# A two-layer fp32 transformer with a sparse third layer: turning between stages by token tile, and inverse roots of the attention heads on VectorE

## The reference, cut to what matters

```
def rms_norm(x, g):
    return x * rsqrt(mean(x * x, -1) + EPS) * g

for i in range(2):
    a = mixer(rms_norm(h, norm_g[i, 0]))              # mla_mixer, then diff_mixer
    h = h + rms_norm(a, norm_g[i, 1])
    f = conv_ffn(rms_norm(h, norm_g[i, 2]))
    h = h + rms_norm(f, norm_g[i, 3])
h = hybrid_layer(h)                                   # begins with rms_norm(h, g_mix)

# in diff_mixer, for each of 8 heads, o is [256, 128]:
    p = softmax(q0 @ k0.T - bias) - lam * softmax(q1 @ k1.T - bias)
    o = rms_norm(p @ v, subln_g) * (1 - lam_init)
```

## Time and profile before

| | us |
|---|---|
| median of 3 runs | 1344.09 |
| lowest, highest | 1343.32, 1346.96 |
| the profiled execution, its time | 1345.34 |
| the profiled execution, its span | 1343.5 |
| TensorE busy in it | 1282.8 |
| GpSimd, ScalarE, VectorE busy | 573.2, 548.0, 509.6 |
| mean granted TensorE clock | 0.994 |

### The profile page before, as it was taken

How to read it: one execution, slowest core, us unless ns; L and a number is a source line. 1 busy time by engine, 2 the same in 40 slices (tenths; PEclk the granted TensorE clock), 3 DMA queues, 4 the chain that set the end, 5 groups by cost and what they waited for, 6 DMA issues and landing times.

```text
span 1343.5 us, 20032 instructions
## 1 busy us (share of the span) xinstructions
PE 1282.8 (95%) x7959; PEld 954.6 (71%) x7959; DVE 509.6 (38%) x1303; ACT 548.0 (41%) x853; POOL 573.2 (43%) x136
## 2 busy tenths in 40 slices
PE   6999999999998899999999999999999999999996
PEld 6867999998987799999878888854444444454442
DVE  2434444445265454444657453421111111121112
ACT  4654555556477465555543664311111111111112
POOL 4722788885944188888567855200000000000001
PEclk9999999999999999999999999999999999999998
DMA  8731666664633266664446444599999999999994
GB/s 270 235 94 63 182 195 188 190 199 144 220 126 95 63 203 196 196 188 165 149 165 203 159 137 161 230 421 426 427 428 428 429 428 429 429 429 428 429 423 189
DMA packets 156933, 341.22 MB, mean 254 GB/s; under 512 B 8537, under 2 KB 119482, under 8 KB 144314
## 3 DMA queue, kind: packets, MB, share of 16 engines
q1 hardware_dynamic: 156858, 340.18, 68.1%
HBM read 339.10 MB, written 1.05 MB: 253 GB/s over the span
## 4 chain that ended last, share of the span: by engine, by line
PE 75%; DMA 13%; ACT 4%; DVE 4%; POOL 2%; issue 1%; SPq 0%; ACTq 0%; DVEq 0%
PE bank L669 16%; PE bank L671 15%; PE bank L670 15%; PE bank L1237 11%; DMA xspare<-in_w 6%; DMA ring<-in_w 6%; PE bank L1262 5%; PE bank L1187 3%; PE bank L768 2%; POOL parts L621 2%; PE bank L679 1%; PE bank L1217 1%; ACT parts L1305 1%; PE bank L1105 1%; PE bank L1121 1%
## 5 line engine op out<-in xcount | busy, mean ns | idle before, releaser
L621 POOL TENSOR_TENSOR parts<-raw,parts 128x2048 fp32r<-128x2048 f32 (+4 forms) x128 | 568.0, 4466 | 290.2 <-ACT parts L1305 290.2
L669 PE MATMUL bank<-xh,parts 128*128 128x256 f32 x1032 | 288.0, 279 | 6.0 <-POOL parts L621 4.0
L670 PE MATMUL bank<-xl,parts 128*128 128x256 f32 x1032 | 285.9, 277 | 0.0
L671 PE MATMUL bank<-xh,parts 128*128 128x256 f32 x1032 | 285.8, 277 | 0.0
L1305 ACT ACTIVATE parts<-raw 128x2048 fp32r<-128x2048 f32 (+4 forms) x128 | 236.1, 1853 | 23.4 <-PE bank L669 8.5
L1237 PE MATMUL bank<-ring,room 128*64 128x512 f32 x768 | 226.1, 594 | 7.1 <-DMA ring<-in_w 4.5
L644 POOL TENSOR_TENSOR xn<-h,gpost 128x512 f32<-128x512 f32 x4 | 4.9, 1270 | 474.7 <-DVE h L2258 474.7
L669 PEld LDWEIGHTS bank<-xh,parts 128*128 128x128 f32 x1032 | 194.2, 188 | 12.6 <-POOL parts L621 4.8
L670 PEld LDWEIGHTS bank<-xl,parts 128*128 128x128 f32 x1032 | 193.8, 188 | 0.8
L671 PEld LDWEIGHTS bank<-xh,parts 128*128 128x128 f32 x1032 | 193.9, 188 | 0.0
L1237 PEld LDWEIGHTS bank<-ring,room 128*64 128x64 f32 x768 | 72.5, 137 | 111.4 <-issue 111.4
(11 more groups left out here) (255 smaller groups left out, 1858.9 us busy)
## 6 DMA issues: line engine op xcount, KB each, us to landing
ring<-in_w SPq DMA_DIRECT2D x67, 2048.0 KB, 22.9
raw<-in_ffn_w_up SPq DMA_DIRECT2D x88, 512.0 KB, 4.9
room<-in_w SPq DMA_DIRECT2D x12, 2048.0 KB, 20.3
raw<-in_ffn_w_down SPq DMA_DIRECT2D x44, 512.0 KB, 3.9
xspare<-in_w SPq DMA_DIRECT2D x11, 2048.0 KB, 26.6
raw<-in_w_in SPq DMA_DIRECT2D x40, 512.0 KB, 4.1
raw<-in_diff_w_qkv SPq DMA_DIRECT2D x24, 512.0 KB, 4.6
ring<-in_w SPq DMA_DIRECT2D x10, 1024.0 KB, 24.8
```

The costliest lines, as they stand in the source:

```text
L621: pool.tensor_tensor(low[:, p % PARTS, 0:n], raw[:, p % RING, 0:n], high[:, p % PARTS, 0:n], ALU.subtract).then_inc(low_ready, 1)
L669: first = pe.matmul(out_, a[0], b[0], start=start, stop=False)
L670: pe.matmul(out_, a[0], b[1], start=False, stop=False)
L671: return first, pe.matmul(out_, a[1], b[0], start=False, stop=stop)
```

## The change

At the turns (all in `build`):
- The outputs are normed and added by token tile: `turned_over` does gain, sum, root and residual of tile 0, then of tile 1 (`post` did both at once). The last `down` of a feed-forward net runs tile 0's products to the end before tile 1's.
- Turns 1 to 3: `h` is not multiplied by root and gain on VectorE and then transposed. VectorE multiplies the identity by the root (`spread_roots`), and TensorE multiplies `h` by that diagonal, which transposes and scales in one matmul (`h_transposed`). The gain, now feature on the partition (`gcol`, loaded by four small DMAs once), goes in as a scale in the copies to the high and low part, which are of 128x256, one per 128 features (`high_chunks`, `low_chunks`). Turn 4 transposes `h` itself.
- TensorE's next product waits for each pair of feature blocks instead of for the first and the second half (`k_tile`).
- `keep_clock` runs 16 matmuls at turns 1 to 3 and 4 at turn 4. Banks of `x4` and `qi` are fixed at 0 to 3.
- The three loads of `gpre` between layers are gone.

In differential attention: Ln and Exp of ScalarE are gone (with their table loads); VectorE makes the roots itself from the bits of the value, in 13 chained instructions on 128x4 (`inverse_roots`).

```
-            def normed(site, by_rows=False):
-                dve.wait_ge(h_squares, 2 * site + 2)
-                refined(st[:, 16:18], st[:, 0:2])
...
-                    dve.scalar_tensor_tensor(dst, src, st[:, 16 + t:17 + t], g, ALU.mult, ALU.mult).then_inc(xn_ready, 1)
+            def root_of(t, y):
+                guesses[0] += 1
+                dve.wait_ge(guessed, guesses[0])
+                dve.wait_ge(vec, steps[0])
+                a = st[:, 48 + t:49 + t]
+                link(dve.tensor_scalar(a, y, y, st[:, 32 + t:33 + t], ALU.mult, ALU.mult))
+                link(dve.tensor_scalar(y, a, 1.5, y, ALU.add, ALU.mult))
...
+                def summed(t):
+                    dve.wait_ge(post_squares, 4 * site + 2 * t + 2)
+                    dve.tensor_tensor(st[:, 18 + t:19 + t], st[:, 2 + 2 * t:3 + 2 * t], st[:, 3 + 2 * t:4 + 2 * t],
+                                      ALU.add).then_inc(sums_ready, 1)
+                    dve.wait_ge(sums_ready, 2 * site + t + 1)
+                    half_of(t, st[:, 18 + t:19 + t])
...
+                gained_half(0, 0)
+                gained_half(0, 1)
+                summed(0)
+                residual(0)
+                gained_half(1, 0)
+                summed(1)
+                gained_half(1, 1)
+                residual(1)
+            def spread_roots(site):
+                for t in range(NT):
+                    dve.wait_ge(h_squares, 2 * site + t + 1)
+                    half_of(t, st[:, t:t + 1])
+                    root_of(t, st[:, 28 + t:29 + t])
+                    dve.tensor_scalar(spread_r[:, t], ident, st[:, 28 + t:29 + t], None, ALU.mult).then_inc(spread_ready, 1)
+            def low_chunks(name, site):
+                for k in range(KT):
+                    g = G[name] + k // 2
+                    x_parts[0] += 1
+                    dve.wait_ge(x_high, x_parts[0] + (1 - k % 2))
+                    ins = dve.scalar_tensor_tensor(xl[:, k, :], bank[BANK[g]][:, S * (k % 2):S * (k % 2) + S],
+                                                   gain_of(site, k), xh[:, k, :], ALU.mult, ALU.subtract)
...
+            def h_transposed(name, site, scaled):
+                b = [begin(G[name] + q) for q in range(4)]
+                for t in range(NT):
+                    if scaled:
+                        pe.wait_ge(spread_ready, 2 * (site - 1) + t + 1)
+                    else:
+                        pe.wait_ge(h_ready, 2 * (site - 1) + t + 1)
+                    for k in range(KT):
...
+                        if scaled:
+                            ins = pe.matmul(dst, src, spread_r[:, t], start=True, stop=True)
+                        else:
+                            ins = pe.transpose(dst, src, ident)
...
+                late.extend([(2 * q, G[name] + q) for q in range(4)])
...
-            WAIT = 32
+            WAIT = 16
...
+            def high_chunks(name, site):
+                for k in range(KT):
+                    g = G[name] + k // 2
+                    full(act, g)
+                    act.activation(xh[:, k, :], bank[BANK[g]][:, S * (k % 2):S * (k % 2) + S], ACT.Copy,
+                                   scale=gain_of(site, k)).then_inc(x_high, 1)
...
-                    act.activation(r, ss_o[:, 2 * hd - 2:2 * hd + 2], ACT.Ln, bias=eps_t[:, 0:1],
-                                   scale=1.0 / P).then_inc(logged, 1)
-                    act.wait_ge(logged, hd // 2 + 1)
-                    act.activation(r, r, ACT.Exp, scale=-0.5).then_inc(guessed, 1)
...
+            def inverse_roots(y, sums):
+                v, a = st[:, 32:36], st[:, 48:52]
+                link(dve.tensor_scalar(v, sums, 1.0 / P, EPS, ALU.mult, ALU.add))
+                link(dve.tensor_scalar(y.bitcast(I32), v.bitcast(I32), 1, None, ALU.logical_shift_right))
+                link(dve.tensor_scalar(y.bitcast(I32), y.bitcast(I32), -1.0, float(0x5f3759df), ALU.mult, ALU.add))
+                link(dve.tensor_scalar(v, v, -0.5, None, ALU.mult))
+                for _ in range(3):
+                    link(dve.tensor_tensor(a, y, y, ALU.mult))
+                    link(dve.tensor_tensor(a, a, v, ALU.mult))
+                    link(dve.scalar_tensor_tensor(y, a, 1.5, y, ALU.add, ALU.mult))
```

More of the change, by code:

```diff
@@ L930, in down @@
                     w = parts(p, 2, D)
[L931 to L937, removed]
-                                                     start and x == 0, stop and x == 1)
-                                behind(first)
-                                if stop and x == 1:
-                                    ins.then_inc(ffn_full, 1)
+                    each = [(x, t, hf) for x in range(2) for t in range(NT) for hf in range(2)]
+                    if stop:
+                        each = [(x, t, hf) for t in range(NT) for x in range(2) for hf in range(2)]
+                    for i, (x, t, hf) in enumerate(each):
+                        if not any(x == y for y, _, _ in each[:i]):
+                            pe.wait_ge(hid_ready, n + (n0 + 1 + x))
+                        first, ins = product(bank[4 + 2 * t + hf][:, :],
+                                             [y[:, (j + x) % 4, t * P:t * P + P] for y in (hh, hl)],
+                                             [y[:, x, 512 * hf:512 * hf + 512] for y in w],
+                                             start and x == 0, stop and x == 1)
+                        behind(first)
+                        if stop and x == 1:
+                            ins.then_inc(ffn_full, 1)
                     owed[0] += 1
@@ new lines, in turned_over, with gained_half, residual @@
+            def turned_over(site, banks, ring_groups):
+                def gained_half(t, hf):
+                    b = banks[2 * t + hf]
+                    dve.wait_ge(post_squares, 4 * site + 2 * t + hf + 1)
+                    x = slice(512 * hf, 512 * hf + 512)
+                    ins = dve.tensor_tensor(xn[:, t, x], bank[b][:, :], gpost[:, x], ALU.mult)
+                    ins.then_inc(bank_moved[b] if ring_groups else vec, 1)
+                    if not ring_groups:
+                        steps[0] += 1
+                def summed(t):
[4 more added lines that the diff above has]
+                    half_of(t, st[:, 18 + t:19 + t])
+                def residual(t):
+                    root_of(t, st[:, 16 + t:17 + t])
+                    for g in (ring_groups or [])[2 * t:2 * t + 2]:
+                        moved(dve, g)
@@ L1943, in mla_beside @@
                     full(dve, g)
+                    dve.tensor_copy(gcol[:, :], bank[BANK[g]][:, 1:1 + 4 * KT])
                     dve.tensor_copy(subT[:, :], bank[BANK[g]][:, 0:1]).then_inc(bank_moved[BANK[g]], 1)
@@ L1948, in _ @@
                 moved(dve, g)
-            post(0, [BANK[G["mla_o"] + n] for n in range(4)], range(G["mla_o"], G["mla_o"] + 4))
+            turned_over(0, [BANK[G["mla_o"] + n] for n in range(4)], range(G["mla_o"], G["mla_o"] + 4))
             def tile(n, b, par):
```

139 lines of the change are left out of this document (69 added, 70 removed).

## The result

The changed kernel takes 1365.52 us (median of four runs, 1364.17 to 1368.11), against 1345.53 us for the kernel before in four runs (1343.32 to 1350.77): 1.0146 times as long, 95% interval 1.0123 to 1.0169. It was forecast slower by 6.1 us, at 1350.2 with a range from 1340 to 1356; it is slower by 20 us, over three times as much. The profiled execution has a span of 1362.4 us, 18.9 more than before, at a mean clock of 0.986.

The account below looks back on a forecast made before the run. TensorE was taken to bound the kernel, holding 75% of the chain. Turns -4.5, pairs of heads +7.6 and clock +3 summed to +6.1 us: a median of 1350.2 us, slower, with an 8-in-10 range of 1340 to 1356.

Parts of the forecast that it names:

- The turns in themselves: At the four turns between layers: gains of 1.7, 0, 1.7 and 2.5 us before turn 4's clock cost.
- turn 4 would be held: In turn 4, VectorE's sum of two SBUF columns at about 646.3 would wait for GpSimd, busy to 646.65.
- The pairs: Differential attention: GpSimd's earlier piece holds VectorE's roots, delaying TensorE by +3.6, +2.2, +2.3 and -0.5 us, sum +7.6.
- 7.6 + 3: Differential attention: 7.6 us from the four pairs of heads plus 3 us of 1.2 GHz spells behind TensorE's idle times.
- small operands don't stand: Rival, VectorE beside GpSimd: only wide instructions are held, sum about -10 us, 1334 us, faster; chance 0.17.
- it stands, but the clock holds: Rival, pairs: TensorE keeps 2.4 GHz or GpSimd misses the third pair; +1.7 us, 1344 to 1347; chance 0.25.
- The clock: 1.2 GHz spells behind TensorE's idle times: 1.4 us at turn 4 and 3 us at the pairs of heads.
- the turns lose too: Rival, turns with 16 fillers: a 1.2 GHz spell on the diagonal's matmuls costs each turn 1.7 us; 1355 us; chance 0.1.
- Turns: -4.5 us: All four turns together, with 1.4 us of clock taken off turn 4's gain: 4.5 us shorter.
- Costed at nothing: the four DMAs of `gcol`, its copy: Loading `gcol`: SP is idle there, TensorE needs it 60 us later, the copy is 0.2 us on VectorE; 0 us.

Follow-up runs that it names:

- e3: Changed kernel with the heads' roots made again by ScalarE's Ln and Exp and VectorE's refinement, turns and `gcol` as changed; 1354.73 us, 1.0064 of before.
- e4: Kernel before with only the changed kernel's thirteen-instruction roots on VectorE added; 1360.03 us, 1.0104 of before.
- e5: Changed kernel with the heads' roots by ScalarE as before and `gcol` placed behind all other tensors; 1346.42 us, 1.0007 of before.
- e1: Changed kernel with `gcol` placed in SBUF behind all other tensors, same instructions; 1357.81 us, 1.0092 of before.
- e9: e5 with more filler matmuls: 24, 30 and 24 in turns 1 to 3, 6 and 9 in turn 4; 1341.37 us, 0.9968 of before.
- e2: Kernel before with an unused tensor of 32 columns (128 bytes) where the change puts `gcol`; 1364.99 us, 1.0136 of before.
- e7: Kernel before with an unused tensor of 64 columns (256 bytes) where the change puts `gcol`; 1346.0 us, run once.
- e12: Kernel before with 32 unused columns ahead of `xh` and 32 more ahead of `hh` (inputs 128 bytes off, hidden values 256); 1354.5 us, run once.

## Why the prediction was wrong

**The turns in themselves: close.** Forecast shorter by 1.7, 0, 1.7 and 2.5 us, measured 2.1, -0.2, 2.1 and 3.0. Turn 2 came out right partly by luck. L1843 was held by GpSimd (1.30 us) as forecast, but the spell of 1.2 GHz cost it as well: in e3, with the same hold (1.33 us) and no spell, turn 2 is 11.23 us long, 0.7 shorter than before. That turn 4 would be held too was wrong (0.15 us at 662.40, GpSimd done at 662.43), and the sum didn't need it.

**The pairs: right.** Roots held from their first instruction in pairs one and two, at the eleventh in pair three, free in pair four; TensorE's waits 5.1 and 5.2 us, forecast 5.2. Differential attention grew by 9.4 us, with the spells of the pairs in it; the working had 7.6 + 3. Between profiled kernels that differ by the roots alone it grew by 10.1 (before to e4), 11.0 (e3 to the changed kernel) and 12.6 us (e5 to e1). Here the pace cost nothing (1.4 us above the fast one in both kernels), so this stretch is a fair test. The rival *small operands don't stand* is refuted by the first instruction of the roots, 3.10 us where it takes 0.16 alone; *it stands, but the clock holds* by the windows.

**The clock: right in kind, short in size.** I took 1.4 us for a spell at turn 4 and 3 for the pairs. There was one more in turn 2, on the matmuls with the diagonal (the clock read 0.57 at 327 to 331), which the rival *the turns lose too* had for each turn, and one at 897. The term "Turns: -4.5 us" was mis-sized by this: without the shift and the roots it measured +1.0 us (e5, -0.5 to +2.4), and -4.3 only with more fillers (e9). e5 and e9 differ by 5 us, by the ratios, for fillers alone.

**The step that failed** is the sentence "Costed at nothing: the four DMAs of `gcol`, its copy". I looked at what `gcol` does and not at where it lies. Its 128 bytes put `xh`, `xl`, `hh` and `hl` 128 bytes off against the weight pieces, and some 3,800 matmuls of the products came at the slow distance, 4.4 ns later, where 1,000 did before: 13.1 us by the trace, 17 to 18 in e2's runs. With this term the sum would have been 6.1 + 13.1 = 19.2, against 20.0 measured, but that it comes out so near is luck: taking the shift away from the changed kernel gave back only some 7 us (e1), whose trace has spells at 1.2 GHz in other places. So the shift, put at nothing, accounts for 7 to 13 of the 14 us that the sum lacked. The rest is most likely the clock's, above all at the turns; its share is not shown more closely.
## What to carry to other kernels

When work is taken off an engine, ask what its next instruction now starts earlier and what that collides with; here 3 us spared on ScalarE became stands of 3.1, 3.1 and 4.5 us on VectorE. Filler matmuls are to be matched to the idle time that is left at each place, not cut by a common factor. Terms that move the clock do not simply add: what one edit gives back in one stretch, a spell at 1.2 GHz can take in the next.

## What the runs showed of the hardware

- Products whose operand lies 128 bytes off (against its place in the kernel before, relative to the weights) come 4.4 ns further apart in the feed-forward nets, with 256 columns (113.3 to 117.7 ns) and with 512 (228.9 to 233.3) alike, at a granted clock of 1.00. 256 bytes change nothing there (e7). Other distances were not run, and the 92 matmuls on `hh` in the hybrid layer (117.8 ns in the kernel before and e7, 113.7 in e12) do not follow this.
- A VectorE instruction on four columns with a single SBUF input stands until GpSimd's instruction ends (3.10 us against 0.16), as does an addition of two single columns (1.30 against 0.15), while L1714 on single columns runs inside one. For the four-column form this was an assumption of mine; the Trainium skill ("SBUF — State Buffer", section "SBUF: two separate sides", with "VectorE: DVE Perf Modes", section "Mode 2×_2P") had it so.
- Idle times of TensorE of 3.0 and 3.5 us behind 3.8 us of fillers were followed by 1.2 GHz (changed kernel and e5, turn 2), while 30 fillers and 0.33 us of idle at the same place were not (e9). In e3 3.02 us of idle behind the same 3.8 us of fillers were not followed by it either, so the length of the idle time alone did not decide it.
